# Routing stage of a diffusion layer: expert choice by match-and-replace, codes by a maximum of eight, gates gathered with the token rows, the shared expert cut into pieces

## The reference

```python
s = sigmoid(xf @ w_router)                      # 640 x 64
sc = s + router_bias
gscore = top_k(sc by 8 groups of 8, 2).sum()    # best 4 groups stay
idx = top_k(where(group stays, sc, -inf), 8)
w = s[idx] / s[idx].sum() * 2.5                 # gates
# tokens sorted by expert; per row: (silu(x @ w_gate[e]) * (x @ w_up[e])) @ w_down[e] * gate
shared = (silu(xf @ ws_gate) * (xf @ ws_up)) @ ws_down
x = x + g2 * (routed + shared)
```

## Time and profile before

| what | value |
|---|---|
| median of 3 runs | 1156.0 us (1154.32 to 1156.79) |
| the profiled execution | 1157.22 us, its span 1155.4 us |
| PE busy | 1051.0 us, 91% of the span |
| DVE busy | 353.1 us, 31% |
| ACT busy | 231.3 us, 20% |
| POOL busy | 190.9 us, 17% |
| DMA | 321.40 MB, mean 278 GB/s |
| chain that ended last | PE 77%, DVE 10%, DMA 8% |

### The profile page before, as it was taken

The page is one execution under the profiler, slowest core; times in us unless marked ns, Lnnn a source line. Parts: engine busy times, 40 slices in busy tenths (PEclk is TensorE's granted clock), DMA queues, the critical chain, the costliest instruction groups (busy, mean ns, idle before and its releaser), DMA issues.

```text
span 1155.4 us, 18176 instructions
## 1 busy us (share of the span) xinstructions
PE 1051.0 (91%) x7307; PEld 457.4 (40%) x7307; DVE 353.1 (31%) x735; ACT 231.3 (20%) x513; POOL 190.9 (17%) x245
## 2 busy tenths in 40 slices
PE   4899999998999567899999999999999999999484
PEld 0455555564455336333333333333333333333132
DVE  0212333764164897011111111111111111111167
ACT  1211104664123110111111211111111111111011
POOL 1000000200313250312212121212212121211000
PEclk9899999999999898999999999999999999999888
DMA  9943339102103300596999999999999999996495
GB/s 376 413 168 146 146 120 276 61 1 92 74 36 115 158 1 0 217 378 251 406 377 335 421 420 421 421 420 419 421 419 411 416 410 421 419 420 262 187 428 244
DMA packets 55884, 321.40 MB, mean 278 GB/s; under 512 B 9492, under 2 KB 10076, under 8 KB 26488
## 3 DMA queue, kind: packets, MB, share of 16 engines
q1 hardware_dynamic: 38976, 271.87, 58.8%
q0 software_dynamic: 14816, 42.03, 9.3%
q10 hardware_dynamic: 2008, 6.33, 1.4%
HBM read 299.45 MB, written 32.28 MB: 287 GB/s over the span
## 4 chain that ended last, share of the span: by engine, by line
PE 77%; DVE 10%; DMA 8%; ACT 2%; issue 1%; SPq 1%; POOL 0%; DVEq 0%; POOLq 0%; ACTq 0%
PE bank L1781 29%; PE bank L1797 15%; PE bank L1432 7%; PE bank L1630 6%; PE bank L1760 4%; DMA ring<-expert_rows 3%; DMA reg_p<-in_w_mod 2%; DMA ring<-in_w_up 2%; PE bank L1421 2%; PE bank L1679 2%; PE bank L1601 2%; PE bank L1459 1%; PE bank L1587 1%; PE bank L1574 1%; PE bank L1526 1%
## 5 line engine op out<-in xcount | busy, mean ns | idle before, releaser
L1781 PE MATMUL bank<-ring,reg_h 128*32 128x512 f32 x2672 | 352.3, 592 | 3.3 <-DVE reg_h L1307 1.2
L1797 PE MATMUL bank<-ring,reg_y 128*32 128x512 f32 x1336 | 181.8, 595 | 1.1 <-ACT reg_y L911 1.1
L1781 PEld LDWEIGHTS bank<-ring,reg_h 128*32 128x32 f32 x2672 | 101.6, 110 | 202.6 <-issue 201.5
L1320 DVE TENSOR_TENSOR reg_h<-reg_h,bank 128x256 f32<-128x256 f32 x51 | 21.5, 422 | 336.9 <-ACT reg_h L927 329.1
L659 POOL DMA_INDIRECT expert_rows<-reg_y,rowc x51 | 51.4, 1008 | 439.8 <-DVE reg_y L1312 427.1
L1781 PE MATMUL bank<-reg_p,reg_h 128*32 128x512 f32 x592 | 119.6, 592 | 0.0
L1432 PE MATMUL bank<-ring,reg_h 128*128 128x384 f32 (+2 forms) x256 | 84.4, 488 | 0.0
L1312 DVE TENSOR_SCALAR reg_y<-bank,reg_p 128x512 f32<-128x512 f32 x51 | 38.3, 751 | 150.3 <-PE bank L1797 150.3
L927 ACT ACTIVATE reg_h<-bank 128x256 f32<-128x256 f32 x51 | 19.6, 384 | 319.0 <-PE bank L1781 319.0
L1797 PEld LDWEIGHTS bank<-ring,reg_y 128*32 128x32 f32 x1336 | 45.5, 109 | 81.7 <-issue 75.4
L1630 PE MATMUL bank<-ring,reg_h 128*128 128x512 f32 x160 | 70.1, 594 | 1.4 <-DVE reg_h L1132 1.4
(11 more groups left out here) (250 smaller groups left out, 1009.9 us busy)
## 6 DMA issues: line engine op xcount, KB each, us to landing
ring<-in_w_gate SPq DMA_DIRECT2D x52, 1024.0 KB, 13.6
ring<-in_w_up SPq DMA_DIRECT2D x52, 1024.0 KB, 20.3
ring<-in_w_down SPq DMA_DIRECT2D x52, 1024.0 KB, 18.0
ring<-in_w_mod SPq DMA_DIRECT2D x21, 1024.0 KB, 6.5
ring<-expert_rows SPq DMA_DIRECT2D x9, 2048.0 KB, 16.1
reg_p<-in_w_gate SPq DMA_DIRECT2D x12, 1024.0 KB, 13.7
reg_p<-in_w_up SPq DMA_DIRECT2D x12, 1024.0 KB, 21.3
reg_p<-in_w_down SPq DMA_DIRECT2D x12, 1024.0 KB, 17.4
```

Of the source, the lines that this page charges most:

```text
L1781: last = pe.matmul(bank[2 + p][R * j:R * j + R, :], xg_t[:, p, k * P + R * j:k * P + R * j + R], w_gu(homes[n % SLOTS])[:, k], start=(k == ...
L1797: last = pe.matmul(bank[5 + hf][R * j:R * j + R, :], h_t[:, p, i * P + R * j:i * P + R * j + R], w_dn(homes[n % SLOTS])[:, i, 512 * hf:512 ...
```

## The change

**Choice.** `route()` finds the chosen groups and experts with `match_replace`, which overwrites the matched values by 1e30: a comparison gives the mask of 64 columns at once. The gates stay in a row of 64 columns per token (`gm`, zero where not chosen), made by a new `gates(t)`: one fused product with its sum, a reciprocal, a scaling. Routes 0 and 1 move behind tiles 2 and 3, route 2 between the halves of tile 4, gates of tile 4 behind the counts. For tile 4 the residual and the shift are added by DVE, not by POOL.

**Codes.** PE sums position, start and a mark of 65536 at each chosen expert in bank 0. DVE adds the place in an extra block where needed, and `max` takes the eight marked values of a token. No one-hots of 8 x 64 are left. Rooms and overflows come from shifts of integers.

**Gates.** The one-hots aren't multiplied by the gate, so the table has 107 columns. A row of `h2_dram` becomes 1088 words: the gates of the token (256 bytes) lie behind its 1024 values, written in one DMA by ACT, and are gathered with it. In each block `block_gates` picks the one of the row's expert, with a column `ecol` that PE makes from a new constant `tiles` (64 x 204). POOL's next gather waits for it (`s_gc`), and so do the scalings.

**Shared expert.** `shared_up` runs in pieces between the small steps of the order and between the tables, and the h transposes apart from the downs. The five downs stand behind the tables and around the transposes of block 0, in banks 0 to 3, 5 and 6, and DVE takes product and sum from PSUM (`shared_sum`). POOL keeps the products of h; the clearing of the gather buffers is gone.

```diff
-        h2_dram = nc.dram_tensor("h2_rows", (NTOK, D), F32, kind="Internal").ap()
+        h2_dram = nc.dram_tensor("h2_rows", (NTOK, ROW), F32, kind="Internal").ap()
...
+            sp.dma_start(tiles[:], tiles_c).then_inc(s_late2, 16)
...
         @block.gpsimd
         def _(pool):
-            def shared_add(pool, t):
-                pool.wait_ge(s_sho, t + 1)
-                out = shared_rows(t)
-                pool.tensor_tensor(out, out, g2bc[:, min(t, 1), :], ALU.mult).then_inc(s_shm, 1)
-                pool.wait_ge(s_shm, t + 1)
-                pool.tensor_tensor(xs[:, t, :], xs[:, t, :], out, ALU.add).then_inc(s_shx, 1)
...
-            for t in range(T):
+            for t in range(T - 1):
...
-            shared_add(pool, 0)
-            shared_h(pool, 3)
-            for t in range(1, T - 1):
-                shared_add(pool, t)
+                pool.tensor_tensor(sg_up[t], sg_up[t], up[:, t % 2, :], ALU.mult).then_inc(s_shh, 1)
...
+            pool.wait_ge(s_gmo, 16)
...
+                    pool.wait_ge(s_gc, b + 1)
...
+                    act.wait_ge(s_shd, t - 1)
                 act.copy(h_t[:, t % 2, :], bank[4][:, 0:2 * P]).then_inc(s_she, 1)
...
+            shared_silu(0)
             shared_silu(1)
+            act.wait_ge(s_gm, T)
+            act.dma_start(h2_dram[:, D:ROW].rearrange("(t p) e -> p t e", t=T), gm).then_inc(s_gmo, 16)
             shared_silu(2)
...
             shared_silu(3)
...
+            shared_h_t(0)
+            shared_silu(4)
+            shared_h_t(1)
+            shared_h_t(2)
...
                 link(last)
                 link(dve.tensor_tensor(gsc[:], g8[:, :, 0], g8[:, :, 1], ALU.add))
                 link(dve.max(top[:], gsc[:]))
...
+                link(dve.tensor_copy(need[:, 0:4], top[:, 0:4]))
+                link(dve.match_replace(gpen[:], need[:], gsc[:], HIT))
+                link(dve.tensor_scalar(gpen[:], gpen[:], HIT, NEG, ALU.is_lt, ALU.mult))
                 link(dve.tensor_tensor(sc[:].rearrange("p (g e) -> p g e", g=8), sc[:].rearrange("p (g e) -> p g e", g=8),
                                        gpen[:].unsqueeze(2).to_broadcast([P, 8, 8]), ALU.add))
                 link(dve.max(top[:], sc[:]))
...
+                link(dve.match_replace(sc_hit, top[:], sc[:], HIT))
                 with nc.allow_low_precision("zeros and ones are exact"):
...
+                    dve.tensor_scalar(maskm[:, t, :], sc_hit, HIT, None, ALU.is_ge).then_inc(s_mm, 1)
+            def gates(t):
+                link(dve.scalar_tensor_tensor(gm[:, t, :], sc_hit, HIT, sig[:, t, :], ALU.is_ge, ALU.mult, accum_out=gsum[:, 0:1]))
                 link(dve.reciprocal(gsum[:, 1:2], gsum[:, 0:1]))
...
+                dve.tensor_scalar(gm[:, t, :], gm[:, t, :], gsum[:, 1:2], ROUTED, ALU.mult, ALU.mult).then_inc(s_gm, 1)
...
+                    if t == T - 1 and hf == 0:
+                        route(T - 3)
+                        gates(T - 3)
+                if t == T - 1:
+                    dve.wait_ge(s_x2, 2 * T)
+                    dve.tensor_tensor(xs[:, t, :], xs[:, t, :], x2_tmp, ALU.add).then_inc(s_x2r, 1)
                 if t:
...
                 if t == T - 1:
+                    dve.wait_ge(s_h2a, T)
+                    dve.tensor_tensor(h2row[:, t % 2, :], h2row[:, t % 2, :], sh2bc[:, cond, :], ALU.add).then_inc(s_h2, 1)
                     h2t_half(t)
...
-                if t and t != T - 2:
-                    route(t - 1)
+                if t in (2, 3):
+                    route(t - 2)
+                    gates(t - 2)
+            route(T - 2)
+            gates(T - 2)
...
             dve.wait_ge(s_start, 1)
...
+            dve.tensor_copy(ends, bank[5][:, 0:E])
+            link(dve.scalar_tensor_tensor(over_i[:], bank[5][:, E:2 * E], P - 1.0, count, ALU.add, ALU.add))
+            link(dve.tensor_single_scalar(over_i[:], over_i[:], 7, ALU.arith_shift_right))
+            link(dve.tensor_scalar(xb[:], over_i[:], 0.0, None, ALU.max))
+            link(dve.tensor_tensor_scan(xinc[:], ones[:, 0:E], xb[:], float(NQ), ALU.mult, ALU.add))
+            dve.tensor_tensor(late, placed, ends.unsqueeze(1).to_broadcast([P, T, E]), ALU.add)
             link(dve.tensor_tensor(xb[:], xinc[:], xb[:], ALU.subtract))
...
+            link(dve.scalar_tensor_tensor(shift, xb[:], float(P), ends, ALU.mult, ALU.add))
+            link(dve.scalar_tensor_tensor(jmap, late, BIG, shift.unsqueeze(1).to_broadcast([P, T, E]), ALU.is_ge, ALU.mult))
+            link(dve.tensor_tensor(jmap, jmap, placed, ALU.add))
             for t in range(T):
...
+                last = dve.max(code[:, t, :], jmap[:, t, :])
+            link(last)
             flat = "p t k -> p (t k)"
             code_i, part_i = row_i[:, 0:T * TOPK], tok_i[:, 0:T * TOPK]
...
+            link(dve.tensor_scalar(code_i, code.rearrange(flat), -BIG, None, ALU.add))
             link(dve.tensor_single_scalar(part_i, code_i, P - 1, ALU.bitwise_and))
             link(dve.tensor_copy(place_f.rearrange(flat), part_i))
             link(dve.tensor_single_scalar(part_i, code_i, 7, ALU.logical_shift_right))
...
+            link(dve.tensor_copy(block_f.rearrange(flat), part_i))
...
+                link(dve.tensor_tensor(blocks, iota[:, 0:NT].unsqueeze(1).to_broadcast([P, TOPK, NT]),
+                                       block_f[:, t, :].unsqueeze(2).to_broadcast([P, TOPK, NT]), ALU.is_equal))
+                dve.tensor_tensor(blocks, blocks, row_f[:, t, :].unsqueeze(2).to_broadcast([P, TOPK, NT]), ALU.mult)
                 dve.tensor_tensor(place, iota.unsqueeze(1).to_broadcast([P, TOPK, P]),
-                                  place_f[:, t, :].unsqueeze(2).to_broadcast([P, TOPK, P]), ALU.is_equal)
-                link(dve.tensor_tensor(blocks[:, :, 1, :], iota[:, 0:NT].unsqueeze(1).to_broadcast([P, TOPK, NT]),
-                                       block_f[:, t, :].unsqueeze(2).to_broadcast([P, TOPK, NT]), ALU.is_equal))
-                link(dve.tensor_tensor(blocks[:, :, 0, :], blocks[:, :, 1, :],
-                                       row_f[:, t, :].unsqueeze(2).to_broadcast([P, TOPK, NT]), ALU.mult))
-                dve.tensor_tensor(blocks[:, :, 1, :], blocks[:, :, 1, :],
-                                  gate[:, t, :].unsqueeze(2).to_broadcast([P, TOPK, NT]), ALU.mult).then_inc(s_oh, 1)
+                                  place_f[:, t, :].unsqueeze(2).to_broadcast([P, TOPK, P]), ALU.is_equal).then_inc(s_oh, 1)
+            link(dve.tensor_scalar(x_cmp, xinc, scal[:, 4:5], None, ALU.is_le))
+            dve.tensor_reduce(x_e, x_cmp, AX, ALU.add).then_inc(s_ecol, 1)
...
+            def shared_sum(t):
+                dve.wait_ge(s_shd, t + 1)
+                at_least(dve, s_shx, t)
+                for hf in range(2):
+                    cols = slice(512 * hf, 512 * hf + 512)
+                    last = dve.tensor_tensor(sh_tmp[:, cols], bank[SHARED_BANKS[t][hf]][:, :], g2bc[:, min(t, 1), cols], ALU.mult)
+                last.then_inc(s_shm, 1)
+                dve.wait_ge(s_shm, t + 1)
+                dve.tensor_tensor(xs[:, t, :], xs[:, t, :], sh_tmp, ALU.add).then_inc(s_shx, 1)
...
+            def block_gates(b, p, expert, gate):
+                dve.wait_ge(s_xt, b + 1)
+                dve.scalar_tensor_tensor(pick[:, p, :], iota[:, 0:E], expert, xg[:, p, D:ROW], ALU.is_equal, ALU.mult,
+                                         accum_out=gate).then_inc(s_gc, 1)
...
+            shared_sum(0)
+            shared_sum(1)
             xt_half(0, 0)
+            block_gates(0, 0, ecol[:, 0:1], gate_s[:, 0:1])
+            for t in range(2, T):
+                shared_sum(t)
...
+            shared_up(0, 0, 2)
...
+            shared_up(0, 2, KD)
...
+            shared_up(1, 0, 2)
+            router(T - 1)
+            shared_up(1, 2, 6)
...
+            pe.wait_ge(s_mm, T - 1)
+            pe.wait_ge(s_re, T - 1)
+            counts(range(T - 1))
+            shared_up(1, 6, KD)
...
+            counts(range(T - 1, T)).then_inc(s_cnt, 1)
+            every = maskm[:].rearrange("p t e -> p (t e)")
+            pe.wait_ge(s_cnt, 1)
+            pe.matmul(bank[0][:, 0:T * E], upper[:], every, start=True, stop=False)
+            pe.matmul(bank[0][:, 0:T * E], marks[:], every, start=False, stop=False)
+            for o in range(T - 1):
+                pe.matmul(bank[0][:, (o + 1) * E:T * E], onesb[:], maskm[:, o:o + 1, :].to_broadcast([P, T - 1 - o, E]),
+                          start=False, stop=False)
+            shared_up(2, 0, 1)
...
+            shared_up(2, 1, 3)
...
+            pe.matmul(bank[5][:, 0:E], ones[0:E, :], by_rank[0:E, 1, :], start=True, stop=True)
+            pe.matmul(bank[5][:, E:2 * E], ones[0:E, :], by_rank[0:E, 0, :], start=True, stop=False)
+            pe.matmul(bank[5][:, E:2 * E], ones[0:E, :], by_rank[0:E, 1, :], start=False, stop=True)
```

(27 more changed lines are left out.)

284 lines of the change are left out of this document (110 added, 174 removed).

## The result

The changed kernel takes 1121.2 us (median of 4 runs, 1117.5 to 1121.5) against 1156.4 us (4 runs, 1154.3 to 1160.4) beside it on the same chip: ratio 0.9681, 95% interval 0.9665 to 0.9698. It is faster, and the forecast of 1119.6 us was 1.6 us low.

A forecast was written before the change was run, and what follows sets the result against it. The loop was taken as bound by TensorE, the DMA right beside it. Profiled 1157.2 us - 38.9 (earlier first gate/up) + 2.5 (DMA) = 1120.8, with the median 1.2 lower: 1119.6 us; range 1112 to 1129.

The forecast's parts named there:

- The stage is TensorE's list: Routing stage, first shared up to first gate/up: TensorE work 74.3 us plus idle 6.0, first gate/up at 439.2, 38.9 earlier.
- route() and match-and-replace: Routing of a tile on DVE: 4.7 us in all instead of 8.0; match-and-replace between 0.2 and 1.0 us.
- The collision in route(1): Routing stage: route(1) lies beside POOL's add for tile 3, which costs DVE 2.1 us.
- DVE 3 us ahead at the tables: One-hot tables: DVE needs 3.2 us per tile, TensorE 3.7, so DVE stays 3 us ahead.
- Collisions of POOL's shared sums: Old routing stage: nearly each 2.3 us POOL add delays a DVE operation; some 9 of 25.3 us behind s_start.
- What the DMA takes back: Expert loop: gathered rows of 4352 instead of 4096 bytes move 1.31 MB more and cost 2.5 us, between 0 and 5.
- B: Rival, routing stage: held by hand-offs, more DVE collisions, or a low clock adding 6 us; 1127 us, chance 0.20.
- C: Rival, loop: DMA takes back more, upper end (2.5 more) and the lost lead of 2.2; 1125 us, chance 0.15.
- D: Rival: routes and tables cheaper, no wait for router 3, nothing lost to the DMA; 1113 us, chance 0.11.
- E: Rival, loop: falls to the DMA's rate as larger gather rows slow all transfers, slower than before; 1160 us, chance 0.02.
- F: Rival, stage: misplaced waits stall in-order TensorE, so most of the 34 us idle stays; 1140 us, chance 0.02.
- The signs named ahead: Trace marks: TensorE busy 74 of 80 us, tables 1.9, codes 5, weight waits 2 to 5 us, q0 +1.3 MB.

The follow-up runs named there:

- four: Changed kernel with router 3 after four eighths of the first shared up instead of two: 1113.4 us, ratio 0.9617 to the kernel before.
- wide_masks: Changed kernel with two unused 512-element VectorE operations (1.75 us) added to each route(), as the old mask cost: ratio 0.9755 to the kernel before.
- whole_last: Changed kernel with the last shared up run whole ahead of the five one-hot tables, not in quarters between them: ratio 0.9708 to the kernel before.
- before_no_pool_sums: Kernel before the change with GpSimd's shared-expert products and adds narrowed to 1 column of 1024: ratio 0.9848 to the kernel before.
- rows_4096: Changed kernel gathering 4096-byte rows, gates written to their own tensor and never fetched: ratio 0.9645 to the kernel before.
- base_after: The changed kernel run once more, unaltered, as yardstick for the variants: 1117.6 us, ratio 0.9649 to the kernel before.
- early_loads: Changed kernel with weights of experts 3 and 4 loaded once the last shared up frees their buffers: ratio 0.9683 to the kernel before.
- bank_wait: Changed kernel with block 0's gate/up no longer awaiting the last shared product, awaited before block 0's down instead: ratio 0.9638 to the kernel before.
- twice: Changed kernel with four useless 512-column matmuls (1.7 us) in TensorE's pause ahead of router 3: ratio 0.9638 to the kernel before.
- four_bank: Changed kernel with the edits of four and bank_wait together: ratio 0.9631 to the kernel before.
- pool_adds: Changed kernel with four unused 1024-column GpSimd adds, about 2.35 us each, after the first shared-expert product: ratio 0.9688 to the kernel before.

## Why the prediction was right

The total is right because two errors of 3 us cancel, and that is luck: the stage is 3.0 us shorter than forecast, and 5.5 us are given back behind it where 2.5 were forecast. The 1.6 us that the forecast is low lie outside the span: 2.7 us around it instead of 1.8, and a median 0.3 us under the profiled execution instead of 1.2. By its own steps:

**The stage is TensorE's list.** Right, as the place of the first gate/up shows, but 3.0 us too long: 80.3 forecast, 77.3 measured. Three terms were off. The list at full clock is 72.1 us (four, clock 1.00), not 74.3, and most of that is downs and tables: I multiplied whole durations, but what follows a shared down starts 3.44 to 3.49 us after it, not 3.7, and what follows a table 1.76 to 1.77 us after it, not 1.9. The clock was left out of the sum, as "no long pause", and took 1.7. Idle was 3.5 us, not 6.0: 2.09 ahead of router 3 (3.0 forecast), 1.38 ahead of block 0 (1.4), none at the last mask (0.4) and none of the 1.2 of hand-offs. -2.2 + 1.7 - 2.5 = -3.0. What was to hide did: all shared sums but the last product lie under the downs.

**route() and match-and-replace.** 4.7 us forecast, 4.4 measured without a collision. Match-and-replace took 0.15 us over 8 and 0.21 over 64 columns behind a load of 0.09: the index search was the right neighbour, the mask reduction five times too dear.

**The collision in route(1).** Right in place and mechanism: one DVE operation beside POOL's add for tile 3, 1.78 us for 0.22, so 1.6 where I took 2.1. The last mask was forecast for 381.3 us and is done at 381.34, the first table for 398.5 and starts at 398.12, codes take 5.0 us for 5.2. The forecast had TensorE wait 0.4 us for the last mask; it is ready 0.1 us before TensorE asks for it, and wide_masks shows that from there each further us of route() counts in full.

**DVE 3 us ahead at the tables.** Right: no table waits, and whole_last, which takes the quarters away, gets 4.2 us of waits.

**Collisions of POOL's shared sums.** Some 9 of the 25.3 us behind s_start and the late last mask were put down to them; before_no_pool_sums gives 7.9 for the former, 4.0 for the latter, and 17.3 us of the stage's 41.9 in all. The other 24.6 weren't each measured: undone alone, the short masks are worth 11.5, the quarters between the tables 4.9, the first pieces 5.3. These don't add up to an account, since each was undone with the others in place. The codes and the narrower tables were not undone at all. The traces give their lengths: without collisions the old codes take 17.4 us and the new ones 5.0, and from the start of a table to what follows it takes 2.90 us before (between the first two tables of before_no_pool_sums, where nothing waits) and 1.77 now, which by estimate is 5.7 us for five. In before_no_pool_sums the first table doesn't wait for the old codes, as TensorE still has downs to do; how much of their 12.4 us the new order would show is open.

**What the DMA takes back.** 2.5 us forecast, as 1.31 MB at q0's price. The bytes came, the price did not (rows_4096), so this step failed in its cause. Something takes back about as much all the same: from the first to the last gate/up it takes 587.1 us in the kernel before and 586.8 in before_no_pool_sums, but 588.9 to 592.7 in the other twelve traces, 590.6 on average. What is longer are waits for weights (1.1 and 0.8 us in the two old loops, 2.4 to 5.2 in the new ones) and the low clock behind some of them. Not its cause: the row length and the lead of experts 3 and 4. The earlier start as such is an unlikely one: before_no_pool_sums starts 16 us earlier than the kernel before and keeps its loop, and wide_masks starts 8.5 us later than the changed kernel and has 592.7, but no trace has a start between 445 and 461 us. Then there are the loop's own edits, each block's multiply by the gathered gate on DVE and the gather waiting for it. That wait hardly moves the gather: it is issued a median of 3.86 us behind the start of its block's gate/up in base_after and 3.85 in the kernel before. Taking these edits out wasn't tried, and the cause of the 3.5 us stays open. The tail, from the last gate/up to the end, is 90.2 us before and 90.3 on average after; the 91.9 of the changed kernel's own trace, which make its give-back 5.5 us, are scatter.

**Rivals.** B's first half is wrong (no hand-off costs) and its second half is half right: a pause does bring the low clock, but only two pauses over 1 us are left, so it costs 1.7 us and not 6. C's mechanisms are the two that rows_4096 and early_loads speak against; its own terms give 1124.3 us, not 1125. D has the routes and tables right, but not the wait for router 3 (2.09 us) nor the loop. E and F didn't occur.

**The signs named ahead.** TensorE busy 73.8 of 77.3 us (74 of 80 forecast), tables at 1.93 (1.9), weight waits 3.0 us (2 to 5), 5.0 us from `s_start` to the first one-hot (5), q0 +1.31 MB (1.3): all there. Between block 0 and the last the only other idle time is 0.83 us ahead of block 1, which stands in the kernel before too (0.9).

## What to carry to other kernels

In a stage where TensorE waits, add to each pause what it can cost behind itself: here the clock added between nothing and 1.6 times the pause again (1.7 us for 2.1 in five traces, 3.4 for the same pause in two, 4.1 for 7.3 more). So filling a pause, with a later piece of other work first, can pay twice what the wait says, as in four (3.4 us for a wait of 1.7), or just the wait, as in bank_wait. Move wide GpSimd operations away from chains of short VectorE operations on the path, and place them by the one operation each will hold up. Sum an engine's list by start-to-start distances, not by durations, and check a forecast of a transfer's price by taking the bytes away, since the right total here had the wrong cause in it.

## What the runs showed of the hardware

- The same pause of 2.08 to 2.09 us ahead of router 3 left the granted clock at 0.80 (its 2.4 GHz level mixed with 1.2 GHz) for the 8.6 us behind it in the changed kernel; the price until router 4 starts was 1.7 us in five traces and 3.4 us in two, nothing between. With the pause cut to 0.36 to 0.38 us (four, twice, four_bank) the clock stayed at 1.00. Pauses of 1.15 to 1.88 us between the tables of whole_last left it at 1.00 as well. The Trainium skill (TensorE: Matmul & The Clock Gate) says that the throttled state is the default and that activity releases it; twice, where useless matmuls in the pause keep the clock at 1.00, agrees.
- Late in the loop a wait of 2.04 us for weights was followed by a gate/up of 8.77 us at clock 0.81; the kernel before had waited 1.12 us there and kept 7.07. The length alone doesn't decide: at the same block waits of 2.03, 2.04 and 2.16 us (rows_4096, changed kernel, wide_masks) were followed by 8.77 us, and waits of 1.95, 2.15, 2.38 and 2.40 (bank_wait, twice, early_loads, four) by 7.07.
- A GpSimd add of 1024 columns held one VectorE operation until it ended: four adds, four long operations in pool_adds. None of them is a maximum-of-eight or a match-and-replace; those keep their times beside a running add.
- VectorE's match-and-replace over 64 columns: 0.09 us load and 0.21 us; over 8 columns 0.15 us.
